# Where an expert unit does its share of a second block's work: four places, or one

## The reference

```python
def reference(x, c, ctx, c_ctx, ..., c_2, ctx_2, ...):
    x = first_block(x, c, ctx, c_ctx, ...)
    return second_block(x, c_2, ctx_2, ...)
```

```python
hid = jax.nn.silu(xblk @ w_gate[e]) * (xblk @ w_up[e])
return hid @ w_down[e]
```

## Time and profile before

| | |
|---|---|
| median of 3 runs | 3270.17 us (3268.65 to 3277.25) |
| the profiled execution | 3265.85 us, its span 3264.0 us |
| PE busy | 2831.3 us, 87% of the span |
| DVE busy | 809.4 us, 25% |
| ACT busy | 471.2 us, 14% |
| POOL busy | 100.1 us, 3% |
| q1, the strips (and the last output) | 655.38 MB, 49.9% of 16 engines' span |
| q0, the quarters and some tables | 99.43 MB, 8.6% |
| cold units of layer 0, layer 1 | from 369 to about 900 us, from 1245 to about 1740 us |

### The profile page before, as it was taken

The page is one execution under the profiler, slowest core; times in us unless marked ns, Lnnn a source line. Parts: engine busy times, 40 slices in busy tenths (PEclk is TensorE's granted clock), DMA queues, the critical chain, the costliest instruction groups (busy, mean ns, idle before and its releaser), DMA issues.

```text
span 3264.0 us, 33783 instructions
## 1 busy us (share of the span) xinstructions
PE 2831.3 (87%) x14090; PEld 1935.0 (59%) x14090; DVE 809.4 (25%) x1922; ACT 471.2 (14%) x984; POOL 100.1 (3%) x192
## 2 busy tenths in 40 slices
PE   6987867878778988887787998889999898899998
PEld 3553323434456855544455885568788654587886
DVE  2333121112222231111302012441554203513002
ACT  2121001012121121110101001330100003301000
POOL 0001010000000000000000110000000000000000
PEclk8897879988889989998899998999999999999999
DMA  9635989999934659999896432214366421143340
GB/s 391 269 139 204 425 322 394 397 373 388 388 132 178 237 200 402 407 407 402 365 405 257 150 123 103 94 52 155 144 268 261 160 94 52 52 155 123 139 151 13
DMA packets 76106, 764.91 MB, mean 234 GB/s; under 512 B 8176, under 2 KB 10992, under 8 KB 35760
## 3 DMA queue, kind: packets, MB, share of 16 engines
q1 hardware_dynamic: 45968, 655.38, 49.9%
q0 software_dynamic: 27136, 99.43, 8.6%
q10 hardware_dynamic: 2848, 7.90, 0.6%
HBM read 759.27 MB, written 3.41 MB: 234 GB/s over the span
## 4 chain that ended last, share of the span: by engine, by line
PE 74%; DMA 16%; DVE 6%; issue 2%; ACT 1%; SPq 0%; POOL 0%; ACTq 0%; DVEq 0%
PE bank L536 71%; DMA ring<-in_stream 13%; DMA work<-in_stream 3%; PE bank L848 1%; PE bank L840 1%; PE bank L540 1%; DVE MX L1925 0%; DVE work L1864 0%; SPq L452 0%; DVE work L1708 0%; DVE work L1697 0%; DVE work L1942 0%; ACT work L1447 0%; ACT work L1377 0%; DVE X L2134 0%
## 5 line engine op out<-in xcount | busy, mean ns | idle before, releaser
L536 PE MATMUL bank<-A,ring 128*128 128x256 f32 (+1 forms) x3088 | 717.2, 392 | 18.0 <-issue 14.1
L536 PEld LDWEIGHTS bank<-A,ring 128*128 128x128 f32 x3088 | 593.3, 193 | 124.5 <-issue 41.0
L536 PE MATMUL bank<-ring,A 128*32 128x512 f32 (+3 forms) x2304 | 430.8, 660 | 131.7 <-DMA ring<-in_stream 121.2
L536 PE MATMUL bank<-work,ring 128*128 128x256 f32 x1696 | 383.2, 384 | 9.6 <-DVE work L1871 6.1
L536 PEld LDWEIGHTS bank<-ring,A 128*32 128x32 f32 (+2 forms) x2304 | 129.7, 134 | 413.6 <-issue 244.3
L536 PE MATMUL bank<-work 128*64 128x128 f32 (+4 forms) x2084 | 342.4, 336 | 26.1 <-issue 9.6
L536 PEld LDWEIGHTS bank<-work,ring 128*128 128x128 f32 x1696 | 324.3, 192 | 59.6 <-DVE work L1871 7.6
L536 PE MATMUL bank<-A,work 128*128 128x256 f32 x1280 | 292.8, 388 | 16.5 <-issue 11.8
L536 PEld LDWEIGHTS bank<-work 128*128 128x128 f32 (+2 forms) x2084 | 252.5, 176 | 83.7 <-issue 46.0
L536 PEld LDWEIGHTS bank<-A,work 128*128 128x128 f32 x1280 | 245.7, 194 | 70.7 <-issue 32.5
L536 PE MATMUL bank<-work,A 128*128 128x256 f32 (+2 forms) x416 | 141.4, 487 | 20.5 <-DVE work L2363 9.3
(11 more groups left out here) (260 smaller groups left out, 1722.7 us busy)
## 6 DMA issues: line engine op xcount, KB each, us to landing
ring<-in_stream SPq DMA_DIRECT2D x312, 2048.0 KB, 12.9
work<-in_stream POOLq DMA_DIRECT2D x182, 512.0 KB, 9.9
X<-in_xt ACTq DMA_DIRECT2D x1, 2048.0 KB, 18.8
spill<-work ACTq DMA_DIRECT2D x3, 512.0 KB, 13.0
work<-spill POOLq DMA_DIRECT2D x3, 512.0 KB, 5.0
tab_sb<-in_tab_a ACTq DMA_DIRECT2D x1, 1120.0 KB, 25.9
X<-in_ctx2t ACTq DMA_DIRECT2D x1, 1024.0 KB, 13.3
out<-X SPq DMA_DIRECT2D x1, 1024.0 KB, 4.8
```

What stands on the lines that cost most here:

```text
L536: return pay(pe.matmul(o, w, x, start=start, stop=stop, tile_position=place), tells)
```

## The change

The share of context steps of a unit is given out in one slot instead of four: slot b, between the up product and the turning. The sum of the shares per unit is the same, 3.5 for a hot and 22 for a cold unit. No other line differs.

```diff
@@ -965,7 +965,7 @@
                 U = l * UNITS + u
                 at, n, c = units()[u]
                 first = FIRST[f"moe{l}"] + 3 * at
-                pace = (0, 0, 0, 3.5) if n == 2 else (5, 5, 5, 7)
+                pace = (0, 3.5, 0, 0) if n == 2 else (0, 22, 0, 0)
 
                 def product(half, ready):
 
```

## The result

| | before | after |
|---|---|---|
| median of 4 runs each | 3270.36 us (3268.65 to 3277.25) | 3471.45 us (3466.41 to 3484.28) |
| ratio, 95% interval | 1 | 1.0617 (1.0584 to 1.0649) |
| span of the profiled execution | 3264.0 us | 3470.5 us |
| PE busy | 2831.3 us, 87% | 2900.9 us, 84% |

What follows compares the result with a forecast made beforehand. Copies bound the expert stages. Units 3 to 7 (51), 11 to 16 (71), unit 2 (28) and the last units (13, 16) sum to +179 us, added to the 3270.17 us median: 3449 us, range 3365 to 3505.

Steps and rivals of the forecast that it cites:

- The loop: Cold unit's period after the change, a serial chain of waits and products: 54.8 us + C, above a 67 us byte floor.
- parts 1 and 2: From ScalarE taking the down product to the next gate product's fourth strip, 12.9 us; then the gate product, 8.1 us.
- parts 3 and 4: From the gate product's release to the fourth up strip, 13.3 us; then the up product, 9.3 us.
- copies still set the steady periods: Rival: ring refills sooner, so units 3 to 7, 11 to 14 and 16 keep their periods; 3341 us, chance 0.1.
- C: PE's time in a unit's slot b block; sums 126.4 us in units 3 to 7, 172.0 in units 11 to 16.
- chains that grow: Rival: blocks wait on one more ScalarE or VectorE turn each step, 4.5 us in 13 units; 3508 us, chance 0.05.
- Quarters: In slot b, four come from store, later ones land 6.1 us apart while PE eats one in 3.4 us.
- quarters in time: Rival: second queue served as asked, blocks at nominal cost plus chains, some 50 us less; 3399 us, chance 0.2.
- Unit 2: First cold unit of layer 0, with rows, columns and two normalisation sums in slot b: 136.3 against 108.6 us, +28.
- The hot units: Each layer's two move one row or merge from slot d to b; 0 taken, 4 us together if cover were missing.
- The last units: Units 8 and 17, after which PE waits for no strip: +16 and +13 us.
- faster: Rival: gate and up strips no longer share copies with quarters, 5.5 us less in 11 units; 3210 us, chance 0.03.

Runs made afterwards that it cites:

- small_one: Changed kernel, but each quarter's copy from the fifth on brings only 16 of 1024 columns: 3367.22 us, 1.0307 to the kernel before.
- half_ad: Kernel before, with cold units' 22 us split as 11 in slot a and 11 in slot d: 3322.78 us, 1.016.
- b14: Kernel before, with cold units given 4, 14, 0 and 4 us in slots a to d: 3328.59 us, 1.0191.
- hot_only: Kernel before, with only the hot units' 3.5 us moved from slot d to slot b: 3282.66 us, 1.0026.
- all_d: Kernel before, with all 22 us of each cold unit in slot d: 3499.67 us, 1.071.
- placed_same: Kernel before, with cold units given 8, 4, 2 and 8 us in slots a to d, same sum: 3279.5 us, 1.0014.

## Why the prediction was right, and where its sum was off

**The loop.** Two strips from issue to landing took 11.96 and 14.12 us against 12.24 and 13.38. From ScalarE taking the down product to the silu of the next gate product there were 22.2 us on average (21.0 in the sum, parts 1 and 2), from there to VectorE's product 22 (22.6, parts 3 and 4), turning to the second half of the down product 10.6 (11.2). Without the blocks, taken here with the 0.6 us up to ScalarE's turning, that is 272.2 us in units 3 to 7 where the sum had 271, and 332.9 in units 11 to 16 where it had 325: the loop itself came out 1.3 us a period too short in layer 1. The copy queue ran dry: from 822.00 to 834.00 us, the turning, gather and down product of unit 6, 1 GB/s moved (last column). The 5 us that the prediction gave for a block of 22 us were seen in unit 3 (block 20.7); after the longer block of unit 11 the queue was dry for about 10 us.

```profile
822.00:834.00 12.00, 11.66 (x99) 6.45 (x97) 0.34 (x2) 3.40 (x9) 0.00 (x0) 0.93 0.01 1
```

By the Trainium skill (DMA: Bandwidth & Descriptors, "Anatomy of one DMA"), which gives its 2.0 us + bytes / 436 GB/s for one copy issued by GpSimd, two strips are 11.6 us, an estimate; the strips are issued by SyncE. With hardly anything but strips moving, small_one took 12.02 for the gate strips, near the rule, and 14.20 for the up strips. In those 14.2 us 5.53 MB moved (389 GB/s), more than the 4.19 MB of two strips, and in the 12.02 us 4.62 MB: strips issued behind the one that was waited for had a part of the copy engines. So the rule is near for the first of the two copies and not for the second, and the sum by the rows was the better one.

That "copies still set the steady periods" (3341) is wrong by this row and by the copy share; half_ad shows the case in which they do.

**C.** This is the term that was mis-sized most. From VectorE's product to ScalarE's turning (C plus 0.6) the blocks took 145.1 us in units 3 to 7 against 129.4 in the sum, and 181.7 against 175.6 in units 11 to 16. Of the 15.7 us in layer 0, 7.8 are in unit 6, and they are the attention steps. The sum took 4.5 us a step, from the earlier trace rows. The timeline of ScalarE in after:

```profile
801.46 0.60 ACT L1372 ACTIVATE work<-bank 128x512 f32<-128x512 f32 x1 [2.06 <-PE bank L540]
...
807.47 0.60 ACT L1372 ACTIVATE work<-bank 128x512 f32<-128x512 f32 x1 [2.06 <-PE bank L540]
```

They come 6.0 us apart. It is not the quarters: in small_one, where none is waited for, the same steps are 6.0 us apart and the block of unit 6 takes the same 32.4 us. What differs in the windows is the granted clock. After from 795 to 821 us, and before at the steps of the earlier trace rows (the clock is the third column from the end).

```profile
795.00:821.00 26.00, 21.81 (x72) 15.03 (x72) 8.24 (x25) 7.06 (x21) 0.00 (x0) 0.53 0.64 272
```

```profile
1006.00:1018.00 12.00, 7.33 (x46) 5.65 (x45) 5.48 (x17) 3.83 (x11) 0.00 (x0) 1.00 0.81 337
```

PE ran almost wholly at 1.2 GHz, after a wait for up strips (14.69 us from issue to landing) and with small matmuls between ScalarE's and VectorE's turns; the steps of the earlier trace rows ran at 2.4 GHz. In b14 the same steps of unit 6 come 4.6 us apart at a clock of 1.00, with PE busy 5.46 us for two of them where small_one has 15.01 us for three at 0.50:

```profile
763.40:772.60 9.20, 5.46 (x34) 3.86 (x33) 4.03 (x12) 3.23 (x10) 0.00 (x0) 1.00 1.00 429
```

```profile
745.60:763.60 18.00, 15.01 (x49) 10.31 (x49) 6.10 (x18) 4.85 (x15) 0.00 (x0) 0.50 0.56 239
```

So the spacing goes with the clock. I had costed a chain by rows from a stretch in which PE ran at the higher level. Units 7 and 5 add 4.1 (attention steps too) and 3.4 us; in unit 5 nv0's quarter took 15.19 us from its issue. Here the direction of the rival "chains that grow" was right in two units out of thirteen (6 and 7), and its reason, one more turn for each step, was not the one seen.

**Quarters.** The step said four from the store and then 6.1 us each, and 6.2 to 6.4 were seen. Its weight in the blocks, 50 us in all by the rival "quarters in time", is 62 in small_one against after, so this too was taken too small. And the kernel as a whole gained 104 us: unit 2 gained 29, unit 1 8, and the strips had the copy engines to themselves. In that rival the transfers stay, though, which no run here shows.

**Unit 2.** 136.3 was predicted, 133.2 came, in part by luck: from the gate product's silu to VectorE's product there were 21.2 us, not the 27.5 that were to stay, while the block agrees (76.9 against 76.6) and the two parts behind it came out 1 us longer each. Within the block, row 8's quarter took 27.22 us from its issue where 20.08 were taken from the earlier trace rows; rows 9 to 11 then had 4.52, 5.91 and 7.07 us, and their products followed at 434.7, 441.5, 450.9 and 461.5, so 6.8, 9.4 and 10.6 us apart where 9.7 were taken, 2 us less in all; the two sums were one behind the other, as said:

```profile
407.48 27.22 DMA work<-in_stream
...
436.96 4.52 DMA work<-in_stream
...
444.96 5.91 DMA work<-in_stream
...
454.41 7.07 DMA work<-in_stream
...
467.33 3.60 DVE work L1697
...
477.02 3.60 DVE work L1708
...
482.75 12.09 PE bank L536 x95
```

**The hot units.** Taken at 0, with "4 us together" if the cover were missing. Unit 1 cost 6.2 us (hot_only: 6.3). The cover was 20 us of copying; what was late was not unit 1's own strips but the release of four slots ahead of unit 2, whose fourth gate strip took 22.23 us from its issue in after, with quarters beside it (13.41 us in small_one, where unit 1 costs 0.7 us). Units 9 and 10 did cost nothing. This step failed, for 6 us of 206.

**The last units.** +14.3 and +11.6 where 16 and 13 were predicted. In unit 17 from VectorE's product to its first addition are 42.0 us (43 predicted), against the 29.0 of the earlier trace rows:

```profile
1900.58 0.69 DVE L2124 TENSOR_TENSOR work<-work,bank 128x512 f32<-128x512 f32 x1 [36.54 <-PE bank L536]
...
1942.57 3.47 DVE L2134 SCALAR_TENSOR_TENSOR X<-bank,MOD,X 128x256 f32<-128x256 f32 x8 [14.11 <-PE bank L536]
```

**The rival "faster".** It was right that the strips land sooner when no quarter travels beside them, and right that the length of the block decides. But in b14 the units with blocks of 10.4 to 14.4 us stayed at 69 to 71 us and gained nothing below it: the copies are the floor there (unit 15 came down to it from 76.5). The prediction also said that only the up product's release gives the copies six strips of work; all_d and half_ad show nothing special in that release, and a block behind the down product's costs no less (222 us against the kernel before beside it; 201 in slot b).

**What stays open.** Why unit 2 costs 7 us and more in every other division of the same or a larger sum (115.7 to 141.0 in place of 108.7), except in hot_only (104.8) and with small quarters. Its rows are of four quarters each, and I did not vary its share alone. The 7 us of placed_same are one profile against one, and may be nothing but the difference between two executions. Nor did I run a kernel with one block and a larger store.

## What to carry to other kernels

Side work that is to hide beside a stream of copies must be cut so that a release of buffers lies between the pieces; two pieces with no release between them cost three quarters of what one long piece does; and each piece should be short against the copies that are queued when it begins (here blocks of up to 14 us cost nothing or little and those from 17 us on did). Between the two single places tried, b and d, the difference was small beside what either cost. Where the copies are the bound and PE idles, more side work in small pieces is the gain (here 2.2% with 28 us and 2.8% with 33), until the periods grow by as much as the work shrinks elsewhere. And a chain of small dependent steps is costed by a row from a stretch with the same clock.

## What was not expected of the hardware

The clock has a part in a change that moves only waits. In units 11 to 16 PE's busy time for the same instructions rose by 26.2 us, in units 3 to 7 by 26.9, as the granted clock fell from 0.90 to 0.85 and 0.82: as much as a third of the 153 us that the steady units lost. How much of it lay on the path no run separates, and some of it was in the sum, through gate and up products costed after a wait.

The clock also differs where the program does not. From 100 to 200 us, ahead of every edit, it was granted at 0.91 in before, but at 0.76 in placed_same (third column from the end in both rows), where PE got through 448 instructions in place of 515, and that profiled execution reached unit 0's silu 13.4 us later. Over the twelve kernels with full quarters this point was reached between 311.2 and 327.5 us.

```profile
100.00:200.00 100.00, 95.54 (x515) 55.54 (x508) 38.94 (x115) 30.62 (x75) 0.00 (x0) 0.91 0.46 189
```

```profile
100.00:200.00 100.00, 98.43 (x448) 52.63 (x440) 34.62 (x102) 25.10 (x64) 0.00 (x0) 0.76 0.46 189
```

So a difference of 10 to 15 us between two single profiles' spans says nothing by itself; the periods of the stage in question say more.

Last, in both windows read with the two queues at work, they shared the copy engines by packets, not by bytes: 320 and 320 packets, 4.62 and 1.18 MB (559 and 558, 8.11 and 2.08 MB in the earlier trace rows). This is the rule of taking turns that the Trainium skill states (DMA: Bandwidth & Descriptors, "Queues, rings and completion order"), and the trace agrees. The strips moved 14.4 KB a packet and the quarters 3.7 KB, so the quarters had a fifth of the bytes in both windows.
